# Block 2: the norms, the output ahead of each and the first two panels behind it in two halves of the tokens

## The chip, the cores and the metric

The kernel runs on one core of a Trainium2 chip. Its engines are PE (matrix engine; its weight loads are shown apart as PEld), DVE (vector), ACT (scalar), POOL and SP, which here only issues transfers; the trace calls the queue of an engine DVEq, SPq and so on. The metric is the device time of one execution in microseconds (us), as the median of several.

## The reference

Two stacks of two transformer layers each, on 512 tokens of width 1024. The first (with 256 context tokens, three attentions and a gate) ends with a norm. The second is what the change touches. Each of its layers:

```python
h = rmsnorm_2(x, norm_mix_g[l]) * (1.0 + sc1) + sh1
u = h @ w_in[l]
# four mixers: attention with decay, pooling, retention, convolution
mix = jnp.concatenate([y_fox, y_pool, y_ret, y_conv], axis=-1)
x = x + g1 * (mix @ w_out[l])

h = rmsnorm_2(x, norm_ffn_g[l]) * (1.0 + sc2) + sh2
f = (jax.nn.silu(h @ ffn_w1[l]) * (h @ ffn_w3[l])) @ ffn_w2[l]
x = x + g2 * f
```

and behind both layers `rmsnorm_2(x, final_g)`. The norm divides each token by the root of the mean of its squares over all 1024 features.

## The kernel before

Activations lie feature by feature: `xl` is 128 partitions (features) by `KC` = 8 chunks by 512 tokens. All weights come as panels of 128 output features (512 KB) through SP. Each is rounded by ACT (`round_panel`, L1176, which waits until a slot of `split` is given back; there are 3), and its rest is made by DVE (`rest`, L1715) or, for the input panels of the second stack, by POOL (`rest2`, L1031). A product is three matmuls for each chunk (high by high, high by low, low by high; `product`, L2216), so a panel of 8 chunks is 24 matmuls of 512 columns. In the first stack an output's weights are two panels of 6 chunks in two slots (L2180 to L2204), in the feed-forward's second product (`w2`) two panels of 6 and 5 chunks in three slots (`W2_CUT`, L2469 to L2483).

The order of the work is written out by hand for each engine; engines meet only through semaphores, and each takes its instructions strictly in its order.

There are five places where a norm stands between an output and what follows: place 0 between the stacks (with two norms at once, the first stack's last and the second's first), place 1 from the mixers' output to the feed-forward in layer 0, place 2 from layer 0 to layer 1, place 3 as place 1 in layer 1, place 4 the last norm. At each of them:

- DVE adds every output to `xl` (`update`, L1937; L1710 in the first stack); ACT squares it (`square`, L1330; `square1`, L1148), POOL adds up the squares of chunks 0 to 6 (`add_square`, L1017).
- PE sums over the features with one-column matmuls (`sum_squares`, L2006; at place 0 `sum_both_squares`, L2017, with 48 passes), first what POOL added up, then the square of the last chunk.
- ACT takes the root, DVE the reciprocal (`over_roots`, L1516), PE spreads it over all partitions (`spread_roots`, L2042).
- `norm_split` (DVE, L1722) multiplies each chunk into `hm2`, a ring of four; `shifted` (ACT, L1337) adds the shift and rounds it into `hs`; the rest of the even chunks is made by DVE (L1736), of the odd ones by POOL (`split_odd`, L1075).
- `first_products` (PE, L2228) multiplies two panels at once with each chunk as it comes. All further panels run alone.
- `norm` (DVE, L1521) is the last norm; SP sends the result in one transfer (L1005).

At places 0 and 2 the first panel gives the forget gate: ACT takes it (L1367), forms its logarithm (L1468 to L1473), DVE a running sum (L1849 to L1853), and then DVE starts 62 steps of the convolution (L1762). Ahead of ACT's take stand, at place 0, POOL's rest of the third panel and four memsets (`pads_done`, L1087 to L1090), and DVE's final norm of the first stack (L1750).

## Time and profile before

| what | us |
|---|---|
| median of three runs | 2600.06 (2599.46 to 2600.43) |
| the profiled execution, whole | 2602.91 |
| its span, first to last instruction | 2601.1 |
| PE busy | 2467.2 (95%) |
| PE weight loads busy | 1989.6 (76%) |
| DVE, ACT, POOL busy | 1328.9 (51%), 938.6 (36%), 538.6 (21%) |

The span is shorter than the execution by 1.8 us. The trace gives for each instruction its start in the span and its length; matmuls are pipelined, so their lengths overlap and only their distances add up. In the groups of rows below, "x8" is the count of instructions in a row, and the bracket says how long the engine stood idle before and who released it. The granted clock is the share of full speed (2.4 GHz) that PE was given; 0.5 is 1.2 GHz.

### The profile page before, as it was taken

The page shows a single profiled execution, that of the slowest core. Times are in us where ns is not written, and L with a number is a line of the kernel's source. Part 1 is how long each engine was busy: PE and PEld are TensorE (multiplying, and loading weights), DVE is VectorE, ACT ScalarE, POOL GpSimd, SP SyncE. Part 2 cuts the span into 40 slices and gives each one's busy share as a digit, 9 for nine tenths or more (in the row PEclk, how much of TensorE's full clock was granted, in tenths as well). Part 3 has the DMA queues.
Part 4 walks back from the last instruction along what each step waited for, and adds up shares of the span by engine and source line. Part 5 has one row for each costly group of instructions (what it writes and reads, how often), then busy time and mean ns, then how long its engine had stood idle before and what let it go on. Part 6 is the DMA issues. An engine that isn't in the chain of part 4 may idle for free.

```text
span 2601.1 us, 37185 instructions
## 1 busy us (share of the span) xinstructions
PE 2467.2 (95%) x14408; PEld 1989.6 (76%) x14408; DVE 1328.9 (51%) x2663; ACT 938.6 (36%) x1686; POOL 538.6 (21%) x512
## 2 busy tenths in 40 slices
PE   6999999999998999999999999999999999999997
PEld 4777877878886678778777657888887667788886
DVE  4567757665306663666717644333334854433333
ACT  4354254452323542545334333222224333322221
POOL 2211222212343122222364231000003232000001
PEclk9899999999998999999999999999999999999999
DMA  6301422125124034132433112323323212223322
GB/s 265 133 1 52 178 76 88 64 86 189 55 94 161 2 122 154 38 130 110 176 103 122 49 54 68 98 79 116 95 80 101 67 49 73 82 82 106 104 77 70
DMA packets 64383, 250.31 MB, mean 96 GB/s; under 512 B 7888, under 2 KB 9424, under 8 KB 54736
## 3 DMA queue, kind: packets, MB, share of 16 engines
q1 hardware_dynamic: 59920, 234.26, 26.9%
q0 software_dynamic: 3776, 13.63, 1.6%
q8 instruction: 115, 1.88, 0.3%
q14 instruction: 60, 0.49, 0.1%
q10 hardware_dynamic: 512, 0.03, 0.0%
HBM read 243.67 MB, written 4.19 MB: 95 GB/s over the span
## 4 chain that ended last, share of the span: by engine, by line
PE 85%; DVE 7%; ACT 4%; issue 2%; DVEq 1%; DMA 0%; POOL 0%; ACTq 0%; SPq 0%
PE ps L2221 37%; PE ps L2078 20%; PE ps L2200 6%; PE ps L560 5%; PE ps L588 5%; PE ps L628 4%; DVE ps L1762 2%; ACT probs L777 2%; PE ps L2059 1%; PE ps L2166 1%; PE ps L2047 0%; PE ps L566 0%; DVE ps L694 0%; PE ps L602 0%; PE ps L638 0%
## 5 line engine op out<-in xcount | busy, mean ns | idle before, releaser
L2221 PE MATMUL ps<-h_split,split_panels 128*128 128x512 f32 x3120 | 742.3, 397 | 10.5 <-DVE h_split L1736 10.0
L2221 PEld LDWEIGHTS ps<-h_split,split_panels 128*128 128x128 f32 x3120 | 590.9, 191 | 146.9 <-issue 25.1
L2078 PE MATMUL ps<-h_split_first,split_panels_first 128*128 128x512 f32 (+1 forms) x2880 | 576.1, 358 | 16.8 <-DVE h_split_first L1649 8.8
L2078 PEld LDWEIGHTS ps<-h_split_first,split_panels_first 128*128 128x128 f32 x2880 | 470.7, 193 | 96.5 <-issue 10.9
L1014 POOL TENSOR_TENSOR split_panels_first<-panels_first,split_panels_first 128x1024 fp32r<-128x1024 f32 (+1 forms) x104 | 232.9, 2240 | 579.4 <-ACT split_panels_first L1174 579.4
L1720 DVE TENSOR_TENSOR split_panels<-panels,split_panels 128x1024 fp32r<-128x1024 f32 (+2 forms) x171 | 191.0, 1117 | 311.6 <-ACT split_panels L1182 309.7
L1182 ACT ACTIVATE split_panels<-panels 128x1024 fp32r<-128x1024 f32 (+2 forms) x210 | 204.2, 974 | 351.3 <-PE ps L2221 350.4
L1601 DVE SCALAR_TENSOR_TENSOR ps<-modulation_panels,silu_c,ps 128x256 f32<-128x256 f32 x480 | 225.2, 487 | 29.7 <-issue 1.3
L2221 PE MATMUL ps<-ffn_hidden_split,split_panels 128*128 128x512 f32 x1056 | 240.0, 389 | 0.0
L2221 PEld LDWEIGHTS ps<-ffn_hidden_split,split_panels 128*128 128x128 f32 x1056 | 198.2, 188 | 41.2
L1022 POOL TENSOR_TENSOR probs<-probs 128x512 f32<-128x512 f32 (+1 forms) x36 | 52.8, 1467 | 781.5 <-ACT probs L1335 781.5
L588 PE MATMUL ps<-matrices,probs 128*128 128x128 f32 x1104 | 154.2, 284 | 23.5 <-ACT probs L777 23.1
L588 PEld LDWEIGHTS ps<-matrices,probs 128*128 128x128 f32 x1104 | 121.6, 143 | 67.3 <-ACT probs L777 44.0
L560 PE MATMUL ps<-qkv 64*128 64x256 f32 (+2 forms) x1168 | 161.4, 388 | 8.3 <-DVE probs_turned L706 2.2
L1174 ACT ACTIVATE split_panels_first<-panels_first 128x1024 fp32r<-128x1024 f32 (+1 forms) x104 | 104.6, 1007 | 119.5 <-PE ps L2200 97.5
L2200 PE MATMUL ps<-gated_rounded,split_panels_first 128*128 128x512 f32 x576 | 144.2, 359 | 3.1 <-ACT gated_rounded L1255 2.4
L560 PEld LDWEIGHTS ps<-qkv 64*128 64x128 f32 x1168 | 103.5, 191 | 48.7 <-issue 23.9
L1034 POOL TENSOR_TENSOR split_panels<-panels,split_panels 128x1024 fp32r<-128x1024 f32 x39 | 95.6, 2453 | 197.0 <-ACT split_panels L1182 197.0
L777 ACT ACTIVATE probs<-ps,row_min 128x512 f32<-128x512 f32 (+6 forms) x192 | 122.6, 649 | 31.3 <-DVE row_min L694 19.7
L805 POOL TENSOR_TENSOR wide_weights<-matrices,row_weight 128x64 f32<-128x64 f32 x240 | 65.3, 294 | 317.0 <-DVE row_weight L712 292.9
L1234 ACT ACTIVATE qkv<-ps 128x512 f32<-128x512 f32 x38 | 36.6, 963 | 247.1 <-PE ps L2078 247.1
L683 DVE TENSOR_REDUCE row_min<-ps 128x1 f32<-128x768 f32 (+5 forms) x144 | 94.1, 671 | 52.2 <-PE ps L560 50.2
(254 smaller groups left out, 2692.7 us busy)
## 6 DMA issues: line engine op xcount, KB each, us to landing
modulation_panels<-in_ada SPq DMA_DIRECT2D x64, 1024.0 KB, 5.0
panels<-in_w SPq DMA_DIRECT2D x88, 512.0 KB, 3.5
panels_first<-in_in SPq DMA_DIRECT2D x72, 512.0 KB, 5.8
panels<-in_in SPq DMA_DIRECT2D x42, 512.0 KB, 3.5
panels_first<-in_out SPq DMA_DIRECT2D x32, 384.0 KB, 3.0
panels<-in_w SPq DMA_DIRECT2D x32, 384.0 KB, 3.0
panels<-in_w SPq DMA_DIRECT2D x32, 320.0 KB, 2.9
panels<-in_out SPq DMA_DIRECT2D x16, 512.0 KB, 3.6
```

The costliest lines, as they stand in the source:

```text
L560: last[e] = nc.tensor.matmul(scores_at(u, e, u["w"][e])[:, col:col + z - a], u["q"][e], u["k"][e][:, a:z], start=True, stop=True, skip_gro ...
L588: ins = nc.tensor.transpose(bank(ev["bank"], at0, at0 + P), probs[:, u["probs_at"], e, col:col + P], ident)
L628: ins = nc.tensor.matmul(bank(b, 0, P)[rows_of(e)], v, turned_slot(ev, 512)[:, at0:at0 + P], start=ev["first"] and j < 2, stop=ev["last"] ...
L777: nc.scalar.activation(probs[:, u["probs_at"], e, 0:w], scores_at(u, e, w), ACT.Exp, bias=row_min[:, s:s + 1], scale=scale, accum_out=row_ ...
L1014: nc.gpsimd.tensor_tensor(flat1(n, 1), raw1[:, n % RAW1, 0:main_size(n)], flat1(n, 0).bitcast(F32), ALU.subtract).then_inc(rest1_done, 1)
L1174: A_(flat1(n, 0), raw1[:, n % RAW1, 0:main_size(n)], ACT.Copy).then_inc(rounded1, 1)
L1182: A_(flat(n, 0), raw[:, n % RAW, 0:panel_size(n)], ACT.Copy).then_inc(rounded, 1)
L1601: ins = V.scalar_tensor_tensor(out=adding if c < KC - 1 else products(k)[:, i, :], in0=w[:, c, :], scalar=v, in1=adding, op0=ALU.mult, op1 ...
L1720: V.tensor_tensor(flat(n, 1), raw[:, n % RAW, 0:panel_size(n)], flat(n, 0).bitcast(F32), ALU.subtract).then_inc(rest_done, 1)
L2078: ins = mm(at0, split1[:, s, w, c, :], hs1[:, h, c, lo:e], start=c == 0 and i == 0, stop=c == KC - 1 and i == 2)
L2200: ins = mm(bank(OUT_BANKS[j][o % 2], 0, e), split1[:, n % SPLIT1, w, c, :], u[:, uc, lo:lo + e], start=uc == 0 and i == 0, stop=uc == MIXC ...
L2221: ins = mm(out, split[:, n % SPLIT, a, c - base, :], moving(b, c), start=first and i == 0 and j == 0, stop=last and i == len(chunks) - 1 a ...
```

## The change

At all five places the 512 tokens are taken as two halves of 256, `h` = 0 and 1:

- The last output (`last_output`) runs all its matmuls on half 0 (256 columns), then on half 1, into two banks. Between the halves come the sums of chunks 0 to 6; at 3/8 of half 1 the sum of the last chunk's squares of half 0, at 3/4 of it the spread of half 0. It needs both panels of the output from its start.
- The last chunk's update, square, root and reciprocal are done per half (`update_half`, `square_half`, `root_half`, `over_half_roots`); those of half 1 lie between the chunks of the norm's half 0.
- `norm_split`, `shifted`, `split_odd` and `first_products` go through all eight chunks of half 0 and then of half 1. The third panel's rounding is put behind chunk 5 of half 0, its rest behind the whole norm (at places 1 and 3 both were ahead of it). At place 2 the second panel is rounded behind the root of half 0, and its rest stands on DVE between the reciprocal and the first chunk. The table of Silu is loaded behind `shifted`.
- At place 0 the sum for the second norm is formed from squares weighted with root(w^2 + eps), made once at the start, so one sum is enough ahead of the norm; the plain sum for the first stack's own norm (16 passes) goes between the halves of the first products, its spread behind them. POOL's `rest2(0, 0)` is moved one step back.
- The last norm goes by halves too, and the result leaves in six transfers: 4 and 4 chunks of half 0, then 2, 2, 2 and 2 of half 1.

```diff
-            sp.wait_ge(result_ready, KC)
-            sp.dma_start(out, xl[:, :, :]).then_inc(result_out, 16)
-            sp.wait_ge(result_out, 16)
+            pieces = [(0, 0, 4), (0, 4, 8), (1, 0, 2), (1, 2, 4), (1, 4, 6), (1, 6, 8)]
+            for h, a, e in pieces:
+                sp.wait_ge(result_ready, KC * h + e)
+                sp.dma_start(out[:, a:e, half_cols(h)], xl[:, a:e, half_cols(h)]).then_inc(result_out, 16)
+            sp.wait_ge(result_out, 16 * len(pieces))
...
+            def square_half(r, h, q, x_count, scale=1.0):
+                if h == 0:
+                    act.wait_ge(sq_added, 6 * q + KC - 3)
+                    act.wait_ge(xh_ready, r + 1)
+                else:
+                    act.wait_ge(x_ready, x_count)
+                A_(squares2[:, (KC - 1) % 2, half_cols(h)], xl[:, KC - 1, half_cols(h)], ACT.Square, scale=scale).then_inc(
+                    sq_ready if h else sq_half, 1)
+            def root_half(r, h):
+                act.wait_ge(sums_half, 2 * r + h + 1)
+                A_(roots[:, 2 * h:2 * h + 2], bank(T_BANK, 2 * h, 2 * h + 2), ACT.Sqrt, bias=EPS if r else tiny[:, 0:1],
+                   scale=1.0 / DM).then_inc(std_half, 1)
...
+            def shifted(r, shift, panel, q, x_count, scale=1.0):
+                for h in range(2):
+                    s = half_cols(h)
+                    for c in range(KC):
+                        act.wait_ge(hm_ready, hm_count(r, h, c))
+                        if c % 2:
+                            A_(hm2[:, c % 4, s], hm2[:, c % 4, s], ACT.Identity, bias=shift(c))
+                            act.drain()
+                            A_(hs[:, 0, c, s], hm2[:, c % 4, s], ACT.Copy).then_inc(hh_ready, 1)
+                        else:
+                            A_(hs[:, 0, c, s], hm2[:, c % 4, s], ACT.Identity, bias=shift(c)).then_inc(hh_ready, 1)
+                        if (h, c) == (0, 1):
+                            square_half(r, 1, q, x_count, scale)
+                        if (h, c) == (0, 3):
+                            root_half(r, 1)
+                            if r == 0:
+                                act.wait_ge(plain_added, KC - 3)
+                                plain_square(KC - 1)
+                        if (h, c) == (0, 5):
+                            round_panel(*panel)
+                        if r == 0 and (h, c) == (1, 1):
+                            act.wait_ge(plain_summed, 1)
+                            A_(roots[:, 4:8], bank(S_BANK, 0, 4), ACT.Sqrt, bias=EPS, scale=1.0 / DM).then_inc(plain_std, 1)
...
+                r = norm_no(l, True)
+                for c in range(KC - 1):
+                    square(DEPTH + r, c, NX1 + l * OUTS2)
                     round_panel(N_IN2 + c + SPLIT, l)
-                root(4 + l * 2, SEQ // P)
+                square_half(r, 0, DEPTH + r, None)
+                root_half(r, 0)
+                shifted(r, lambda c: mod2[:, l, 24 + c:25 + c], (FFN_AT + SPLIT - 1, l), DEPTH + r, NX1 + l * OUTS2 + KC)
                 load_table(ACT.Silu)
-                shifted(4 + l * 2, lambda c: mod2[:, l, 24 + c:25 + c])
...
+            def update_half(r, h, at0, gate, ready, count):
+                s, c = half_cols(h), KC - 1
+                dve.wait_ge(ready, count)
+                old = xl[:, c, s] if r else x1[:, c, s]
+                V.scalar_tensor_tensor(out=xl[:, c, s], in0=bank(at0)[:, s], scalar=gate, in1=old,
+                                       op0=ALU.mult, op1=ALU.add).then_inc(x_ready if h else xh_ready, 1)
...
+            def norm_split(r, gain, shift, at0, gate, count, panels):
+                over_half_roots(r, 0)
+                for p in panels[:-1]:
                     rest(*p)
+                for h in range(2):
+                    s = half_cols(h)
+                    dve.wait_ge(rstd_half, 2 * r + h + 1)
+                    for c in range(KC + 1):
+                        if c < KC:
+                            if c >= 5 and c % 2:
+                                dve.wait_ge(*h_done2(r, h, c - 4))
+                            V.scalar_tensor_tensor(out=hm2[:, c % 4, s], in0=xl[:, c, s], scalar=gain(c), in1=rstd_half_in(h),
+                                                   op0=ALU.mult, op1=ALU.mult).then_inc(hm_ready, 1)
+                        if c % 2:
+                            dve.wait_ge(hh_ready, hm_count(r, h, c - 1))
+                            V.scalar_tensor_tensor(out=hs[:, 1, c - 1, s], in0=hm2[:, (c - 1) % 4, s], scalar=shift(c - 1),
+                                                   in1=hs[:, 0, c - 1, s].bitcast(F32), op0=ALU.add, op1=ALU.subtract).then_inc(h_even, 1)
+                        if (h, c) == (0, 1):
+                            update_half(r, 1, at0, gate, out_ready, count)
+                        if (h, c) == (0, 4):
+                            over_half_roots(r, 1)
+                        if r == 0 and (h, c) == (1, 4):
+                            dve.wait_ge(plain_std, 1)
+                            V.reciprocal(roots[:, 4:8], roots[:, 4:8]).then_inc(plain_over, 1)
+                dve.wait_ge(*h_done2(r, 1, KC - 1))
+                rest(*panels[-1])
...
-            dve.drain()
-            norm(3 + 2 * DEPTH, xl, lambda c: vec("final_g", c), xl, result_ready)
+            over_half_roots(r, 0)
+            for h in range(2):
+                s = half_cols(h)
+                dve.wait_ge(rstd_half, 2 * r + h + 1)
+                for c in range(KC):
+                    V.scalar_tensor_tensor(out=xl[:, c, s], in0=xl[:, c, s], scalar=vec("final_g", c), in1=rstd_half_in(h),
+                                           op0=ALU.mult, op1=ALU.mult).then_inc(result_ready, 1)
+                    if (h, c) == (0, 1):
+                        update_half(r, 1, 4, mod2[:, DEPTH - 1, 40 + KC - 1:40 + KC], out_ready, out1_done + DEPTH * OUTS2)
+                    if (h, c) == (0, 5):
+                        over_half_roots(r, 1)
...
+            def sum_most(q):
+                pe.wait_ge(sq_added, 6 * q + KC - 2)
+                    mm(bank(T_BANK, t, t + 1), square_sum2[:, P * t:P * t + P], ones[:, 0:1], start=t == 0, stop=False, skip_group_check=True)
+            def sum_last(r, h):
+                if h:
+                    pe.wait_ge(sq_ready, KC * (DEPTH + r) + KC)
+                else:
+                    pe.wait_ge(sq_half, r + 1)
+                for t in (2 * h, 2 * h + 1):
+                    ins = mm(bank(T_BANK, t, t + 1), squares2[:, (KC - 1) % 2, P * t:P * t + P], ones[:, 0:1], start=False, stop=True,
+                             skip_group_check=True)
+                ins.then_inc(sums_half, 1)
+            def spread_half(r, h):
+                pe.wait_ge(over_half, 2 * r + h + 1)
+                for i in range(2):
+                    ins = mm(rstd_half_in(h)[:, P * i:P * i + P], roots[:, 2 * h + i:2 * h + i + 1].to_broadcast([P, P]), ident,
+                             start=True, stop=True)
+                ins.then_inc(rstd_half, 1)
+            def last_output(r, q, at, factors, first_panel=0, first_used=None):
+                for h in range(2):
+                    for i, (w, moving) in enumerate(factors):
+                        ins = mm(bank(at[h])[:, half_cols(h)], w, moving[:, half_cols(h)], start=i == 0, stop=i == len(factors) - 1)
+                        if h and i + 1 == first_panel:
+                            ins.then_inc(first_used, 1)
+                        if h and i == len(factors) * 3 // 8:
+                            sum_last(r, 0)
+                        if h and i == len(factors) * 3 // 4:
+                            spread_half(r, 0)
+                    if h:
+                        ins.then_inc(out_ready, 1)
+                    else:
+                        ins.then_inc(out_half2, 1)
+                        sum_most(q)
...
+            pe.wait_ge(rest1_done, N_MAIN)
+            pe.wait_ge(x_ready, KC * DEPTH - 2)
+            last_output(0, DEPTH, (4, 3), [(split1[:, part, w, c, :], u[:, MIXC // 2 * part + c, :]) for part in range(2)
+                                           for c in range(MIXC // 2) for w, u in ((0, u_hi), (1, u_hi), (0, u_lo))],
+                        3 * MIXC // 2, out_half)
...
+            def first_products(banks, panels, r, signals, l):
+                for h in range(2):
+                    s = half_cols(h)
+                    for c in range(KC):
+                        pe.wait_ge(*h_done2(r, h, c))
+                        for at0, n, signal in zip(banks, panels, signals):
+                            if (h, c) == (0, 0):
+                                split_wait(n, l)
+                            for j, (a, b) in enumerate(((0, 0), (0, 1), (1, 0))):
+                                ins = mm(bank(at0)[:, s], split[:, n % SPLIT, a, c, :], hs[:, b, c, s], start=c == 0 and j == 0,
+                                         stop=c == KC - 1 and j == 2)
+                            if (h, c) == (1, KC - 1):
+                                ins.then_inc(signal, 1)
+                        if (h, c) == (0, 1):
+                            sum_last(r, 1)
+                        if (h, c) == (0, 4):
+                            spread_half(r, 1)
+                        if r == 0 and (h, c) == (0, KC - 1):
+                            sum_plain()
...
+                        if (f, c) == (1, KC - 1):
+                            r, i = norm_no(l + 1, False), PER2 - len(W2_CUT)
+                            split_wait(i, l)
+                            split_wait(i + 1, l)
+                            last_output(r, DEPTH + r, (3, 4), [(split[:, (i + j) % SPLIT, w, k - a, :], act_part(b, k))
+                                                               for j, (a, e) in enumerate(W2_CUT) for k in range(a, e)
+                                                               for w, b in ((0, 0), (0, 1), (1, 0))],
+                                        3 * W2_CUT[0][1], w2_used)
+                            break

```

## Rows read from the trace of the kernel before

**Rows 1.** The page: the chain that ended last, shares of the span by engine

```profile
PE 85%; DVE 7%; ACT 4%; issue 2%; DVEq 1%; DMA 0%; POOL 0%; ACTq 0%; SPq 0%
```

**Rows 2.** Timeline of place 2: start us, us, engine, line, operation, [idle before <- releaser]

```profile
1976.90 0.95 PE L2010 MATMUL ps<-matrices,probs 128*128 128x1 f32 x8
1977.10 0.75 DVE L1940 SCALAR_TENSOR_TENSOR x_latent<-ps,mod_second,x_latent 128x512 f32<-128x512 f32 x1 [1.03 <-PE ps L2221]
1978.56 0.97 PEld L2013 LDWEIGHTS ps<-matrices,probs 128*128 128x128 f32 x8 [0.80 <-ACT probs L1335]
1981.29 1.41 DVE L1732 SCALAR_TENSOR_TENSOR probs<-x_latent,gain_second,ps 128x512 f32<-128x512 f32 x2 [1.25 <-PE ps L2047]
1983.72 13.54 PE L2221 MATMUL ps<-h_split,split_panels 128*128 128x512 f32 x48 [2.48 <-DVE h_split L1736]
1996.62 0.68 ACT L1367 ACTIVATE values_forgetting<-ps,layer_vectors 4x512 f32<-4x512 f32 x1 [5.15 <-PE ps L2221]
```

**Rows 3.** A stretch behind place 2, PE alone: stretch, us, busy (count), granted clock

```profile
1983.70:1989.00 5.30, 5.28 (x13) 0.52 0.00 0
```

**Rows 4.** Groups by shape: line, engine, operation, count | busy us, mean ns

```profile
L1643 DVE SCALAR_TENSOR_TENSOR probs<-qkv,gain_first,ps 128x256 f32<-128x256 f32 x16 | 7.6, 473 | 0.0
...
L1298 ACT ACTIVATE h_split_first<-probs,mod_first 128x256 fp32r<-128x256 f32 x8 | 3.9, 493 | 0.0
...
L1079 POOL TENSOR_TENSOR h_split<-probs,h_split 128x512 fp32r<-128x512 f32 x16 | 20.6, 1289 | 57.1 <-ACT h_split L1346 57.1
L1045 POOL TENSOR_TENSOR h_split_first<-probs,h_split_first 128x768 fp32r<-128x768 f32 x8 | 14.6, 1830 | 35.6 <-ACT h_split_first L1295 35.6
```

**Rows 5.** Timeline of place 1

```profile
1608.00 0.95 PE L2010 MATMUL ps<-matrices,probs 128*128 128x1 f32 x8
...
1610.60 1.23 DVE L1720 TENSOR_TENSOR split_panels<-panels,split_panels 128x1024 fp32r<-128x1024 f32 x1 [1.64 <-ACT split_panels L1182]
1616.89 1.04 DVE L1736 SCALAR_TENSOR_TENSOR h_split<-probs,mod_second,h_split 128x512 fp32r<-128x512 f32 x1
...
1628.25 0.60 ACT L1494 ACTIVATE probs<-ps 128x512 f32<-128x512 f32 x1 [5.34 <-PE ps L2221]
```

**Rows 6.** Two streams on the chain (start us, us), and a group of the page

```profile
583.99 8.44 PE ps L2078 x48
952.10 5.71 PE ps L2078 x24
...
L2221 PEld LDWEIGHTS ps<-h_split,split_panels 128*128 128x128 f32 x3120 | 590.9, 191 | 146.9 <-issue 25.1
```

**Rows 7.** Place 0: one line of the chain in order of time, then the timeline

```profile
1351.82 8.39 PE ps L2200 x36
...
1352.93 1.85 POOL L1014 TENSOR_TENSOR split_panels_first<-panels_first,split_panels_first 128x768 fp32r<-128x768 f32 x1
...
1382.60 2.39 POOL L1034 TENSOR_TENSOR split_panels<-panels,split_panels 128x1024 fp32r<-128x1024 f32 x1
1386.10 0.68 ACT L1367 ACTIVATE values_forgetting<-ps,layer_vectors 4x512 f32<-4x512 f32 x1 [4.83 <-POOL decay_of_keys L1090]
1391.77 0.63 ACT L1473 ACTIVATE values_forgetting<-values_forgetting 4x512 f32<-4x512 f32 x1
1392.89 0.67 DVE L1849 SCALAR_TENSOR_TENSOR values_forgetting<-values_forgetting 4x512 f32<-4x512 f32 x1
```

**Rows 8.** Timeline of place 4; SPq is the queue of SyncE

```profile
2584.69 0.95 PE L2010 MATMUL ps<-matrices,probs 128*128 128x1 f32 x8
...
2594.47 0.35 SPq L1005 DMA_DIRECT2D out_features<-x_latent  x1
```

**Rows 9.** The page: DMA issues, KB each, median us to landing

```profile
panels<-in_in SPq DMA_DIRECT2D x42, 512.0 KB, 3.5
...
panels<-in_w SPq DMA_DIRECT2D x32, 320.0 KB, 2.9
...
out_features<-x_latent SPq DMA_DIRECT2D x1, 2048.0 KB, 6.2
```

250 lines of the change are left out of this document (123 added, 127 removed).

## The prediction

> **What bounds the kernel now.** I read the shares of the chain that ended last first: 85% of it is the matrix engine (PE) [rows 1], so time is gained only where PE waits, or at the two ends. The change touches five places: place 0, between the blocks; places 1 and 3, mixing to feed-forward; place 2, layer 0 to layer 1; place 4, the end. The timeline of place 2 shows the pattern [rows 2]. The last output is done at 1976.90, where the sums of squares begin on PE. Update (DVE), square (ACT), sum (PE, 1978.56), root (ACT), reciprocal (DVE) and spread (PE) follow strictly after one another; the norm starts on DVE at 1981.29 and the first product at 1983.72: 6.8 us, of which PE is at sums and spreads for about half. Then PE pays again: the granted clock is 0.52 over the first 5.3 us of the products, nearly all of it at 1.2 GHz [rows 3]. In that time some 12 matmuls are done where 23 would be at full speed, a loss of 2.5 us. Place 1 is alike: the sums start at 1608.00, and the first two panels are through at about 1628.75 (ACT takes the first of them at 1628.25, and three matmuls are still to come behind it) [rows 5]. Place 4 is a chain without cover: 2584.69 to the end of the span at 2601.1 [rows 8]. Place 0 starts at 1351.82 + 8.39 = 1360.2 [rows 7]. J below is the instant at which the last output is done, and J' the same after the change.
>
> **Halved matmuls.** No stream of 256-column matmuls with a load each is in the trace. A stream of pairs (512 and 256 columns, a load each) takes 8.44 us for 48, 0.352 a pair; 24 of 512 columns take 5.71, or 0.238 each [rows 6]. So a half costs 0.114, half of a whole, as long as its own weight load fits under it. The nearest row for the load alone is eight loads with one-column matmuls behind them: 0.97 us, the last one's own 0.19 included, so (0.97 - 0.19) / 7 = 0.111 apart [rows 2]. That just fits. Bounds: 0.111, the load alone, up to 0.19, the length of one load record [rows 6], if none were hidden. I take 0.115, since the pairs are the nearer row, and nothing for the halving.
>
> The Trainium skill speaks against this ("TensorE: Matmul & The Clock Gate", "Back-to-back issue gap"): sustained spacing 131 ns at 512 columns and 81 ns at 128, so two halves would cost clearly more than one whole. By interpolation that is about 98 ns a half, an estimate from that page, and 65 ns more for each split matmul, 22 us for the 342 of them. The row of 0.238 for 512 columns disagrees with its first figure already.
>
> **The last output in halves (places 1 to 4).** PE's own work is the same, but its 24 one-column and spread passes now lie elsewhere: eight passes between the halves (0.95), four behind 3/8 of the second half (0.45), four spreads behind 3/4 of it (0.5). So the output ends 1.9 us later, at J' = J + 1.9. The prices are of one-column passes and spreads 0.111 each [rows 2]. Covered: from the end of the first half, update and square take 1.0 (two ops of 256 columns, 0.473 and 0.493 [rows 4]), and the sum is asked for 0.95 + 1.2 us in: no wait. From the end of the sums (1978.56 + 0.97) to the norm on DVE (1981.29) it was 1.8, the eight spreads (1.0 at least) among it: 0.8 for root and reciprocal, and nine half matmuls (1.0) cover them. Small waits are left: at places 1 and 3 DVE has the rest of a panel (1.23 [rows 5]) ahead of the first half's update and may still be at it, so the update starts up to 1.2 late and PE waits some 0.3. J' = J + 2.2 there, and with hand-overs J + 2.0 at places 2 and 4.
>
> **The norm in halves.** DVE can start 0.55 us before J'. Prices at 256 columns: DVE 0.473, ACT 0.493, and POOL's rest 0.75, extrapolated from 1.289 at 512 and 1.830 at 768 [rows 4]. The loop of two chunks: DVE norms one chunk (0.51 with the hand-over), ACT shifts it (0.53), DVE makes its rest (0.41 to 0.56: at full width such an op took 1.04 with POOL at work [rows 5], where the update took 0.75 [rows 2]), then the next two. That is 1.45 to 1.6 us for two chunks, where at full width it was up to 1.41 + 1.04 = 2.45 [rows 2, 5]; I take 1.6, since POOL is at work in every such loop. PE needs 12 x 0.115 = 1.4 for the same two chunks, so **the producers now set the pace, not PE**. First half: 4 x 1.6, and 1.7 for the panel's rounding (1.0), the second half's square, root and update: 8.1. Second half: 4 x 1.6 and 1.2 for the last odd chunk's way over ACT's copy (no longer than its shift, 0.49) and POOL (0.75): 7.6. So POOL is done at J' - 0.55 + 15.7 = J' + 15.1, PE's last chunk at J' + 15.9. The clock matters little now: PE has slack of 0.2 a pair and some at each hand-over. Only if it fell for 4 to 5 us would PE lag by about 2, and it would catch up more than half of it.
>
> **Places 1 and 3.** The rest of the third panel was made before the norm (1610.60, 1.23) [rows 5]; now it stands behind it on DVE: J' + 15.1 + 1.3 = J' + 16.4, 0.5 later than PE's last chunk. The third panel starts at J + 2.2 + 16.4 = J + 18.6; before, 1628.75 - 1608.00 = 20.75. Gain 2.1 each. The table load for Silu is also put behind the norm, 1.5 us on ACT, which ends as the first product arrives: nothing. What SP loads behind that panel is asked for some 15 us later, but is used five panels (28 us) on.
>
> **Place 2.** Two rests stand in the way: that of panel 1 (1.23) is on DVE between the reciprocal and the first chunk, and can only be rounded once the first w2 panel is given back (2.2 before J'). DVE starts at J' + 0.35, 0.9 later than elsewhere. ACT takes the first product at J' + 16.6 = J + 18.6; before 1996.62 - 1976.90 = 19.7 [rows 2]. Gain 1.1. Everything to the attention follows from that instant (logarithm, then the convolution on DVE), so it arrives whole.
>
> **Place 0.** Here the change adds a wait. The last output now needs both of its panels before it starts. The second panel's slot is given back by the output before (PE starts the last output at 1351.82), then ACT rounds and POOL makes the rest (1352.93, 1.85), ready at 1354.8 [rows 7]. Before, it was wanted 4.2 us into the output. Now PE stands for 3.1 us. Everything on PE is behind it. J' = J + 1.9 + 3.1 = J + 5.0. The plain sum (16 passes, 1.8) goes between the halves and ACT waits for it after two chunks: 2 us more, POOL's end at J' + 17.1. Then as before rest (2.39), memsets (1386.07 less 1384.99, 1.1), ACT's take: J' + 20.7, and the logarithm 6.3 later (1386.10 to 1392.40) [rows 7]: J + 32.0. Before, DVE went on at 1392.89, J + 32.7. Gain 0.7. What went: 48 passes, most of them at the slow clock; what came in: the stall and the slower producers. The loads behind x_ready start 5 us later; a panel of 512 KB lands in 3.5 us at the median, the 2048 KB of the result in 6.2 [rows 9], and this one is due 4 us after its issue: bounds 0 to 2 us, and I take 0 by the row of its own size. DVE's final norm (5.36) starts at J' + 19.3 and is done before the logarithm.
>
> **Place 4.** J' = J + 2.0 = 2586.7. DVE starts 0.75 before it, does two chunks (0.43 each, 0.473 less the overlap that 1.41 for two whole ones shows), update to J' + 0.7, four chunks, reciprocal, two chunks to J' + 3.5, second half 8 x 0.43 to J' + 7.0. The last of six transfers is 256 KB. Before, one of 2048 KB ran from its issue at 2594.47 to the end of the span, 6.6 us, 6.2 of them to landing [rows 8, 9]. The nearest in size, 320 KB, lands in 2.9 [rows 9]: J' + 7.0 + 2.9 + 0.4 = 2597.0. Gain 4.1. Pieces cut to runs of 256 tokens, and six in one queue, are not in the trace. All six together move what the one moved in at most 6.2 us, the first of them from J' + 1.7 on, so even at that rate they are through at J' + 8 or 9. Bounds: 3 (the queue backs up by 1 us) to 4.7 (a smaller piece lands sooner).
>
> **Sum.** 0.7 + 2.1 + 1.1 + 2.1 + 4.1 = 10.1 us. Profiled execution 2602.91 (span 2601.1 and 1.8 around it) to 2592.8; the median of the runs, 2600.06, is 2.85 below the profiled one, so 2589.95, say 2589.9. At 1.45 a pair each of places 0 to 3 gains 1.2 more: 2585. At 1.75, 1.2 less: 2594.6.
>
> **The rivals.** Weight loads that do not hide (slower): some 300 half matmuls of the last outputs and 384 of the first products. On the last outputs each nanosecond counts; on the first products only what is above the producers' 0.133. At 0.19 that is 300 x 0.075 + 384 x 0.057 = 44 us, time 2634. It decides from about 0.14 on, where 300 x 0.025 + 384 x 0.007 = 10.2 eat the gain. Against it stand the 0.352 a pair and 0.111 a load. The page named above would come out on this side: chance 0.06. Producers slower than I have it (hand-overs, POOL and DVE in each other's way, the loads at place 0): 1.8 to 1.9 a pair, 1.6 to 2.4 less at four places, 2597: 0.19. Faster producers, 1.45 a pair and the full 4.7 at the end: 2584: 0.13. That it does not do what it says, the clock still dropping, at place 0 because PE now stands for 3.1 us just ahead of dense work: 2 us there, 0.7 at the others, 2594: 0.07. My forecast: 0.55.
>
> **How the numbers follow.** Likeliest time 2589.9. The range of 2583 to 2598 takes in faster and slower producers and leaves out the weight loads and the tails. Within 0.2% (5.2 us, about what a measurement of this kernel tells from no change) begins at 2594.9: faster takes my forecast, the faster producers, the clock case and a quarter of the slower producers, 0.80; same most of the rest of those, 0.14; slower 0.06.
>
> **What would show it.** Right: granted clock 1.0 through places 1 to 3; the norm's first chunk on DVE before PE's last half matmul; chunks 1.6 us a pair; PE waiting for POOL and DVE within the first products; 3.1 us of waiting for the last panel's rest at place 0; last transfer issued 10 us behind J. Wrong: half matmuls over 0.13 apart, a PE wait inside the last output's second half, a transfer at the end landing 4 us after its issue.

## The result, and the profile after

The changed kernel takes 2582.29 us (median of five runs, 2578.97 to 2586.53), the kernel before 2599.66 us beside it (2599.46 to 2600.43): a ratio of 0.9935, with a 95% interval of 0.9921 to 0.995. It is faster by 17.4 us where 10.1 were forecast, and lies 0.7 us below the range. The profiled execution takes 2582.29 us, with a span of 2580.4.

The page of the changed kernel: the slices of the granted clock, and the chain that ended last. Above it stands the slice row of the kernel before.

```profile
PEclk9899999999998999999999999999999999999999
```

```profile
PEclk9999999999998999999999999999999999999999
...
PE 82%; DVE 7%; ACT 5%; issue 3%; POOL 2%; DVEq 1%; DMA 1%; ACTq 1%; SPq 0%; POOLq 0%
```

POOL is new on the chain with 2% [rows 1 has 0%], 47 us. Only 6.7 of them are rests of the halved norms (L1103), for which PE now waits. The larger part are rests of the first stack's panels (L1035, 20.1) and squares (L1046 and L1053, 15.2), most of them under the last outputs ahead of place 0, where the chain runs over POOL instead of PE and an output takes 8.40 us as before. The timeline of place 1 answers [rows 5]:

```profile
1599.32 0.88 DVE L1810 SCALAR_TENSOR_TENSOR probs<-x_latent,gain_second,ps 128x256 f32<-128x256 f32 x2 [1.25 <-PE ps L2142]
1600.92 0.98 PE L2382 MATMUL ps<-h_split,split_panels 128*128 128x256 f32 x6 [1.04 <-DVE h_split L1814]
...
1608.48 0.86 DVE L1810 SCALAR_TENSOR_TENSOR probs<-x_latent,gain_second,ps 128x256 f32<-128x256 f32 x2
1608.98 0.51 ACT L1395 ACTIVATE h_split<-probs,mod_second 128x256 fp32r<-128x256 f32 x1
1609.53 0.49 DVE L1814 SCALAR_TENSOR_TENSOR h_split<-probs,mod_second,h_split 128x256 fp32r<-128x256 f32 x1 [0.18 <-ACT h_split L1395]
1609.94 0.86 DVE L1810 SCALAR_TENSOR_TENSOR probs<-x_latent,gain_second,ps 128x256 f32<-128x256 f32 x2
...
1613.39 0.74 POOL L1103 TENSOR_TENSOR h_split<-probs,h_split 128x256 fp32r<-128x256 f32 x1 [0.72 <-ACT h_split L1393]
1614.16 1.23 DVE L1795 TENSOR_TENSOR split_panels<-panels,split_panels 128x1024 fp32r<-128x1024 f32 x1 [1.22 <-POOL h_split L1103]
```

```profile
1615.44 0.73 PE L2365 MATMUL ps<-h_split,split_panels 128*128 128x512 f32 x2 [0.27 <-DVE split_panels L1795]
```

The last output is done at 1599.87, so the norm starts 0.55 ahead of its end, two chunks follow two chunks by 1.46 (1608.48, 1609.94), and the third panel starts at 1615.44. At place 2, ACT's take is at 1981.67, 25.2 us behind DVE's update with the seventh output (1956.46); before it was 27.0 ([rows 2] has the take at 1996.62, the update was at 1969.61):

```profile
1966.16 0.87 DVE L1810 SCALAR_TENSOR_TENSOR probs<-x_latent,gain_second,ps 128x256 f32<-128x256 f32 x2
...
1981.67 0.68 ACT L1425 ACTIVATE values_forgetting<-ps,layer_vectors 4x512 f32<-4x512 f32 x1 [1.53 <-PE ps L2382]
```

Place 0: POOL's rest of the second panel, PE's wait for it, and the granted clock behind the wait (columns as in [rows 3], with all engines):

```profile
1346.06 1.81 POOL L1035 TENSOR_TENSOR split_panels_first<-panels_first,split_panels_first 128x768 fp32r<-128x768 f32 x1
...
1347.92 0.79 PE L2152 MATMUL ps<-gated_rounded,split_panels_first 128*128 128x256 f32 x2 [2.97 <-POOL split_panels_first L1035]
```

```profile
1600.90:1606.20 5.30, 5.08 (x39) 4.71 (x39) 3.74 (x10) 4.52 (x11) 2.21 (x3) 1.00 0.00 0
1347.90:1353.70 5.80, 5.78 (x27) 5.78 (x28) 0.00 (x0) 2.01 (x2) 4.77 (x3) 0.50 0.00 0
```

The upper row is place 1, at full clock. The lower is place 0: 27 half matmuls in 5.8 us, at 1.2 GHz from the first.

**Where the time went.** I cut both traces at instants that exist in both: DVE's update with the seventh of eight outputs ahead of each place, DVE's first operation of the convolution, and the end of the span. Place 1 and 3 are taken together with the feed-forward part behind them. The two profiled executions stand first; the other rows are experiments, told below, and a_same is the changed kernel once more.

| us | to place 0 | place 0 | mixing, layer 0 | place 1 + FFN | place 2 | mixing, layer 1 | place 3 + FFN | place 4 |
|---|---|---|---|---|---|---|---|---|
| before | 1351.86 | 46.16 | 204.67 | 366.93 | 38.47 | 201.69 | 367.63 | 23.70 |
| after | 1344.99 | 47.30 | 199.83 | 364.34 | 36.68 | 203.38 | 364.59 | 19.31 |
| a_same | 1353.48 | 46.22 | 199.62 | 364.35 | 36.68 | 201.64 | 364.59 | 19.32 |
| b_setup | 1346.94 | 46.17 | 201.80 | 366.76 | 38.23 | 201.97 | 366.90 | 23.74 |
| b_shift | 1343.05 | 46.19 | 200.61 | 367.64 | 38.35 | 201.67 | 367.60 | 23.70 |
| b_fill | 1350.43 | 46.18 | 200.74 | 365.31 | 36.70 | 200.13 | 365.29 | 24.99 |
| b_mix_fill | 1346.63 | 46.20 | 197.55 | 367.56 | 38.34 | 198.78 | 366.86 | 23.69 |
| a_by_panels | 1344.16 | 42.38 | 199.51 | 364.34 | 36.65 | 201.61 | 364.63 | 19.31 |
| a_one_transfer | 1346.93 | 47.31 | 199.92 | 364.36 | 36.67 | 203.32 | 364.62 | 22.80 |
| a_rest_at_once | 1349.09 | 47.36 | 199.76 | 364.35 | 37.26 | 200.17 | 364.35 | 19.29 |
| a_no_copy | 1350.92 | 43.24 | 200.02 | 362.87 | 35.24 | 200.25 | 362.86 | 19.30 |
| a_early | 1347.68 | 42.35 | 200.68 | 364.94 | 37.66 | 201.33 | 365.21 | 18.90 |
| a_mix_fill | 1349.92 | 42.39 | 198.29 | 364.33 | 36.67 | 197.07 | 364.64 | 19.30 |

From the first two rows: the five places gain -1.14 + 2.59 + 1.79 + 3.04 + 4.39 = **10.7 us**. The other 10.0 us lie in three stretches in which the change does nothing: 6.9 ahead of place 0, 4.8 in the mixing of layer 0, and -1.7 in that of layer 1. So the question for the chip was what these 10 us are.

### The profile page after: what moved, and what is told of

It is laid out like the page before. It is cut to its first block, busy times and chain, and to the rows that moved or that the text cites. A ratio compares the mean times of both kernels' runs of the same rounds, so it can differ in the third digit from the quotient of the medians.

```text
span 2580.4 us, 37996 instructions
## 1 busy us (share of the span) xinstructions
PE 2453.9 (95%) x14734; PEld 1992.7 (77%) x14734; DVE 1338.6 (52%) x2730; ACT 950.7 (37%) x1745; POOL 542.1 (21%) x527
## 4 chain that ended last, share of the span: by engine, by line
PE 82%; DVE 7%; ACT 5%; issue 3%; POOL 2%; DVEq 1%; DMA 1%; ACTq 1%; SPq 0%; POOLq 0%
PE ps L2365 34%; PE ps L2219 21%; PE ps L567 5%; PE ps L595 5%; PE ps L635 4%; PE ps L2341 4%; DVE ps L1850 2%; ACT probs L784 2%; PE ps L2152 1%; PE ps L2200 1%; POOL split_panels_first L1035 1%; PE ps L2307 1%; PE ps L573 0%; DVE ps L701 0%; PE ps L2382 0%
## 5 line engine op out<-in xcount | busy, mean ns | idle before, releaser
L2365 PE MATMUL ps<-h_split,split_panels 128*128 128x512 f32 x2928 | 691.2, 395 | 4.1 <-ACT values_forgetting L1425 2.8
L2365 PEld LDWEIGHTS ps<-h_split,split_panels 128*128 128x128 f32 x2928 | 549.8, 189 | 130.7 <-issue 16.5
L1035 POOL TENSOR_TENSOR split_panels_first<-panels_first,split_panels_first 128x1024 fp32r<-128x1024 f32 (+1 forms) x104 | 233.3, 2243 | 574.6 <-ACT split_panels_first L1220 574.6
L2365 PE MATMUL ps<-ffn_hidden_split,split_panels 128*128 128x512 f32 x990 | 225.1, 389 | 0.0
L2365 PEld LDWEIGHTS ps<-ffn_hidden_split,split_panels 128*128 128x128 f32 x990 | 185.8, 188 | 38.6
L1046 POOL TENSOR_TENSOR probs_turned<-probs_turned,probs 128x512 f32<-128x512 f32 x30 | 41.8, 1394 | 771.2 <-ACT probs L1382 771.2
L2341 PE MATMUL ps<-gated_rounded,split_panels_first 128*128 128x512 f32 (+1 forms) x552 | 136.4, 357 | 3.1 <-ACT gated_rounded L1301 2.4
```

Of the source, the lines that this page charges most:

```text
L1035: nc.gpsimd.tensor_tensor(flat1(n, 1), raw1[:, n % RAW1, 0:main_size(n)], flat1(n, 0).bitcast(F32), ALU.subtract).then_inc(rest1_done, 1)
L2341: ins = mm(bank(OUT_BANKS[j][o % 2], 0, e), split1[:, n % SPLIT1, w, c, :], u[:, uc, lo:lo + e], start=uc == 0 and i == 0, stop=uc == MIXC ...
L2365: ins = mm(out, split[:, n % SPLIT, a, c - base, :], moving(b, c), start=first and i == 0 and j == 0, stop=last and i == len(chunks) - 1 a ...
```

## The experiments

Two theories on the 10 us. **A**: where PE waits or has little to do, the granted clock may or may not fall to 1.2 GHz behind it; which of these falls happen is dealt anew in each execution. **B**: the change removes something fixed there.

### a_same: the changed kernel once more

> The changed kernel as it is, once more, on this chip. Against the kernel before it gained 17.4 us where 10.1 were forecast, and its runs lie 7.6 us apart (2578.97 to 2586.53) where those of the kernel before lie 1.0 apart. Theory A (the clock is dealt anew): the surplus comes from stretches outside the five places in which the granted clock is 1.2 GHz in one kernel's execution and 2.4 in the other's. Then the intervals inside the places (from the end of the last output to the third panel, about 17.5 us at place 1) repeat to 0.3 us here, the total lies somewhere in 2577 to 2588, a longer run has a lower mean clock, and the stretches at 1.2 GHz outside the places are not all the same as in the first profile (those at about 130, 670, 780, 1030, 1245, 1430, 2030 and 2130 us). Theory B (the surplus is fixed work saved): the same stretches and the same total to 0.5 us.

2582.71 us (2580.04 to 2587.76, four runs); before 2596.75 beside it, now from 2591.74 to 2603.05 in 25 runs, ratio 0.9945 (0.9924 to 0.9967). The table: places 1 to 4 repeat to 0.01 us (with their FFN), but the stretch ahead of place 0 takes 1353.48 instead of 1344.99, with the same code. Theory A holds, and B falls. Another chip is no rival: a_by_panels to a_no_copy below ran on one chip with the same code up to place 0, and took 1344.16 to 1350.92 us to it. The kernel before scatters too, by 11 us, and a slower run has a lower mean clock: over its 41 later runs on three chips the two have a correlation of -0.8, from 2588.78 us at 0.979 to 2601.0 and more at 0.972. Its five runs beside the first comparison lie within 1 us; why they lie so close is not shown. Their mean of 2599.9 is 2.4 above that of the 25 (2597.4).

Place 0 is dealt anew as well. The same wait of 2.97 stands there, but in the 5.8 us behind it 36 half matmuls run instead of 27:

```profile
1356.40:1362.20 5.80, 5.79 (x36) 5.80 (x37) 0.00 (x0) 1.99 (x2) 4.77 (x3) 0.71 0.00 0
```

### b_setup: the kernel before with the change's set-up operations

```diff
+ act.wait_ge(tiny_set, 1)
+ A_(weights_of_squares[:, :], weights_of_squares[:, :], ACT.Sqrt, bias=EPS)
...
+ V.tensor_tensor(weights_of_squares[:, :], vec("final_w", 0, KC), vec("final_w", 0, KC), ALU.mult)
```

> The kernel before with nothing but the small set-up operations of the change (a product of 8 columns on DVE, its root on ACT, a tile of 8 columns; nothing reads them). In the trace of the changed kernel 7.1 us of the gain are there by 1230 us, before any of its five places; this asks whether the set-up code carries them. Theory A (the clock is dealt anew by any small displacement): the total moves by some us in either direction, 2593 to 2606, and the difference is seen in stretches at 1.2 GHz, not in work. Theory B (the set-up itself saves them, for instance by another alignment): 2593 and the same stretches gone as in the changed kernel (about 85, 230 and 345 us). Theory C (nothing of either): 2600 and the same stretches as before.

2595.51 us (2591.49 to 2600.63), ratio 0.9996 (0.9985 to 1.0007). The set-up does not carry the gain: theory B's saving of 7 us is excluded by the interval, which leaves 3.9 us at most. Theory A expected the single executions to move, which they do (1346.94 ahead of place 0), but of its "in either direction" the median shows nothing either: over ten runs the deals even out.

### b_shift: the kernel before, started later

```diff
+ for i in range(5):
+     pool.memset(silu_rows, 0.0)
+     pool.drain()
  pool.memset(silu_rows, 0.0).then_inc(silu_zeros, 1)
+ pool.wait_ge(silu_zeros, 1)
+ pool.sem_inc(late_start, 1)
...
+ sp.wait_ge(late_start, 1)
```

> The kernel before with five more memsets of 0.3 us ahead of the first transfer, so that all starts about 1.6 us later and nothing else is changed. Theory A (the clock is dealt anew by any small displacement): the total is not 1.6 us above the kernel before; it lies anywhere from 2593 to 2607, with a mean clock other than 0.971. Theories B and C (the losses belong to fixed places of the program): 2601.7, mean clock 0.971, the same stretches at 1.2 GHz 1.6 us later.

2595.35 us (2590.85 to 2599.24), ratio 0.9995 (0.9982 to 1.0007). The profiled execution is 12.3 us shorter in its span than that of the kernel before (2588.8 against 2601.1), although it starts 2.5 us later (its first transfer at 3.26 instead of 0.75). Here is one stretch of the same work, first in the kernel before, then 6 us earlier in b_shift, then in the changed kernel (there the 10 us start about 2 us earlier in the work):

```profile
225.00:235.00 10.00, 7.70 (x56) 5.42 (x53) 5.21 (x19) 3.73 (x11) 1.63 (x6) 0.83 0.01 2
```

```profile
219.00:229.00 10.00, 7.71 (x65) 5.59 (x64) 5.75 (x22) 3.96 (x11) 1.63 (x6) 1.00 0.01 2
```

```profile
219.00:229.00 10.00, 7.30 (x67) 4.77 (x66) 5.31 (x23) 5.49 (x16) 2.18 (x8) 1.00 0.01 2
```

With the code before, the clock falls in this stretch in one execution and not in the other. So the 6.9 us are not the change's: over five traces with the code before, the way to place 0 takes 1347.8 us in the mean, over eight with the changed code 1348.4. PE's first matmul starts at 16.13 to 18.77 in them, so of the 10.4 us between the shortest and the longest way at most 2.6 are the start.

### b_fill: idle matmuls in the waits of places 1 to 3

```diff
+ def fill(n, q):
+     for i in range(n):
+         still = act_part(0, 0) if q == 4 else mix_part(0, 0)
+         mm(bank(5), still[:, 0:P], still, start=True, stop=True)
...
+ if q in (3, 4, 5):
+     fill(4, q)
  pe.wait_ge(sq_ready, KC * q + KC)
...
  sum_squares(3 + l * 2, SEQ // P)
+ fill(3, 3)
  spread_roots(4 + l * 2, SEQ // P)
+ fill(9, 3)
...
```

Place 2 gets `fill(3, 4)` and `fill(9, 4)` in the same way: 16 idle matmuls at each of the three places.

> The kernel before, with 16 idle matmuls of 512 columns (0.238 us each, 3.8 us in all) put where PE only waits at places 1, 2 and 3: 4 ahead of the last square's sums, 3 ahead of the spreads, 9 behind them; they write a bank that nobody reads. It keeps PE at work through the gap and changes nothing else. The prediction had 2.5 us of each of these places as the price of products at 1.2 GHz behind a gap. If so: granted clock 1.0 in the first products, the first product is taken by ACT 17.2 us after the last output's end at place 2 instead of 19.7, and the kernel takes 2592.5 (3 x 2.5 less), up to 1 us more where a filler is still in the way. Rival: the pace of the producers bounds these products anyhow, so that the clock costs under 1 us a place: 2598 or more.

2593.5 us (2584.82 to 2596.47, ten runs), ratio 0.9979 (0.9967 to 0.9991), which is 5.5 us less where 7.5 were expected (the two medians lie 3.3 apart, the means 4.5, and the interval of 2.3 to 8.6 us holds all of these; the places below decide). Place 2, the stretch that [rows 3] shows at 0.52 (here from the first long stream on), and ACT's take:

```profile
1976.80:1982.10 5.30, 4.99 (x21) 3.85 (x22) 4.61 (x7) 5.05 (x8) 2.61 (x2) 1.00 0.00 0
```

```profile
1974.16 2.32 PE L2010 MATMUL ps<-ffn_hidden_split 128*128 128x512 f32 x9
...
1976.88 1.63 PE L2229 MATMUL ps<-h_split,split_panels 128*128 128x512 f32 x6 [0.40 <-DVE h_split L1736]
...
1987.90 0.68 ACT L1367 ACTIVATE values_forgetting<-ps,layer_vectors 4x512 f32<-4x512 f32 x1 [3.26 <-PE ps L2229]
```

ACT's take comes 17.95 us behind the last output's end (1969.95), where 17.2 were expected and 19.7 stood before. The fall is gone at all three places. Against the other traces of the code before, place 1 with its FFN is 1.9 us shorter (365.31, where the other four have 367.2 in the mean), place 2 1.6 (36.70 and 38.35), place 3 2.0 (365.29 and 367.2), 5.5 in all: the clock's price was **1.6 to 2.0 us a place**, not 2.5. At full clock PE waits for the producers within these products (0.23 for POOL at 1978.74), which it did not at 1.2 GHz. Place 4, which has no filler, took 1.3 us longer in this trace: a fall of the clock met its sums and spreads, and eight spreads take 2.07 instead of 1.16. And at place 2 the filled kernel is as fast as the halved one, 36.70 and 36.68. There the halves bring nothing that a running PE does not; at places 1 and 3 they bring 0.7 to 1.0 more. A reason would be that the rest of the third panel stands behind the norm there and no longer ahead of it; that wasn't tried by itself.

### a_by_panels: place 0 without the wait

Shortened; the new order stands in a function of its own. In it the sum for the first half stands behind 5/9 of the second panel's second half, and the spread behind its last matmul.

```diff
- pe.wait_ge(rest1_done, N_MAIN)
+ pe.wait_ge(rest1_done, N_MAIN - 1)
...
- for h in range(2):
-     for i, (w, moving) in enumerate(factors):
+ for a, e in ((0, first_panel), (first_panel, n)):
+     if a:
+         pe.wait_ge(rest1_done, N_MAIN)
+     for h in range(2):
+         for i, (w, moving) in enumerate(factors[a:e], a):
```

> The changed kernel, with place 0's last output made panel by panel: first panel for both halves of the tokens, then second panel for the first half, then for the second half (72 half matmuls as before; only their order). The second panel is then not wanted until 4.2 us into the output. The prediction put 3.1 us of waiting here; the trace of the changed kernel shows 2.97, and behind it 5.8 us (in the second execution 3.3) in which a half matmul takes 0.213 instead of 0.118. If the wait is the cause of both: no wait ahead of the output, granted clock 1.0 from its start, norm on DVE 10.4 us behind the start of the wait (72 x 0.117 + 1.9 for the passes) instead of 14.1 to 15.2, place 0 shorter by 3.7 to 4.8, kernel 2578 to 2579 against 2582.5. Rival: what follows (the rest of the second panel on POOL, the tables and loads asked for behind x_ready) sets the end of place 0 anyhow, and it gets under 1 us shorter.

2579.69 us (2574.45 to 2582.64), ratio 0.9936 (0.9917 to 0.9954). Place 0 takes 42.38, 4.9 less than in the first trace of the changed kernel and 3.8 less than in the second, where 3.7 to 4.8 were expected. The output runs at full clock, and the norm starts 10.4 us behind its first matmul (1343.96):

```profile
1344.20:1350.00 5.80, 5.80 (x52) 5.80 (x51) 0.71 (x1) 3.99 (x5) 5.80 (x5) 1.00 0.00 0
```

```profile
1354.37 0.87 DVE L1810 SCALAR_TENSOR_TENSOR probs<-x_latent,gain_second,ps 128x256 f32<-128x256 f32 x2 [0.92 <-PE ps L2142]
```

### a_one_transfer: the result in one piece

```diff
- for h, a, e in pieces:
-     sp.wait_ge(result_ready, KC * h + e)
-     sp.dma_start(out[:, a:e, half_cols(h)], xl[:, a:e, half_cols(h)]).then_inc(result_out, 16)
+ sp.wait_ge(result_ready, 2 * KC)
+ sp.dma_start(out, xl[:, :, :]).then_inc(result_out, 16)
```

> The changed kernel, with the result leaving in one transfer of 2048 KB behind the last chunk instead of six. The prediction had the last of six landing 2.9 us behind its issue, the one 6.2. If so, place 4 gets 3.3 us longer. Rival: six transfers of 256-token runs in one queue are no faster in all than the one, and the end is set by the queue: under 1 us.

2587.0 us (2582.43 to 2590.87), place 4 22.80 against 19.31: 3.5 us, as expected. Its one transfer is issued at 2578.94 and the span ends at 2585.9. The DMA issues of the changed kernel over its last 11 us show that six in a queue don't hold each other up:

```profile
out_features<-x_latent SPq DMA_DIRECT2D x2, 512.0 KB, 3.0
out_features<-x_latent SPq DMA_DIRECT2D x4, 256.0 KB, 2.8
```

Of the 4.4 us of place 4, 3.5 are thus the transfers and 0.9 the halves.

### a_rest_at_once: the third panel's rest without its wait

```diff
- dve.wait_ge(*h_done2(r, 1, KC - 1))
  rest(*panels[-1])
```

> The changed kernel, without DVE's wait for POOL's last chunk ahead of the rest of the third panel. In the trace PE waits 0.27 us for that rest at place 1 (and 0.68 at place 2, where ACT's take of the first product is the event that counts). If the wait is what puts it so late: rest on DVE about 1.2 us earlier, third panel on PE 0.3 earlier at places 1 and 3, nothing at place 2. Rival: the rest beside POOL's last chunk slows POOL or itself (1.23 to more than 2), and PE's last chunk comes later.

One run, 2583.58 us. Place 1 with its FFN stays at 364.35, place 3 is 0.2 us shorter, place 2 0.6 us longer: the rival. DVE's rest and POOL's last chunk now run side by side, and POOL's takes 1.29 instead of 0.74:

```profile
1983.83 1.21 DVE L1795 TENSOR_TENSOR split_panels<-panels,split_panels 128x1024 fp32r<-128x1024 f32 x1
...
1984.34 1.29 POOL L1103 TENSOR_TENSOR h_split<-probs,h_split 128x256 fp32r<-128x256 f32 x1 [0.72 <-ACT h_split L1393]
```

### a_no_copy: one ACT operation less for each odd chunk

```diff
- if c % 2:
-     A_(hm2[:, c % 4, s], hm2[:, c % 4, s], ACT.Identity, bias=shift(c))
-     act.drain()
-     A_(hs[:, 0, c, s], hm2[:, c % 4, s], ACT.Copy).then_inc(hh_ready, 1)
- else:
-     A_(hs[:, 0, c, s], hm2[:, c % 4, s], ACT.Identity, bias=shift(c)).then_inc(hh_ready, 1)
+ A_(hs[:, 0, c, s], hm2[:, c % 4, s], ACT.Identity, bias=shift(c)).then_inc(hh_ready, 1)
```

> The changed kernel, with the shift of the odd chunks left out of their rests: ACT rounds them in one operation like the even ones, instead of shift, drain and copy, so the rests of the odd chunks are wrong. It asks which engine sets the pace of 1.46 us for two chunks, where the prediction had 1.6 and DVE. In a pair ACT is busy 0.51 + 0.49 + 0.42 = 1.42, DVE 0.86 + 0.49 = 1.35, PE 12 x 0.117 = 1.40. If ACT sets it: 1.40 or DVE's 1.38 a pair, and places 1 to 3 each 0.4 shorter. If DVE or the hand-overs between DVE and ACT set it: 1.46 stays to 0.02.

One run, 2576.57 us. The kernel leaves out the shift in the rests of the odd chunks. Neither expectation is met whole. The pace stays at 1.46 (1608.12, 1609.58, 1611.03), as in the last line of the expectation, with ACT now idle 0.55 in each pair:

```profile
1608.12 0.86 DVE L1805 SCALAR_TENSOR_TENSOR probs<-x_latent,gain_second,ps 128x256 f32<-128x256 f32 x2
...
1608.63 0.91 ACT L1390 ACTIVATE h_split<-probs,mod_second 128x256 fp32r<-128x256 f32 x2 [0.55 <-DVE probs L1805]
1609.17 0.49 DVE L1809 SCALAR_TENSOR_TENSOR h_split<-probs,mod_second,h_split 128x256 fp32r<-128x256 f32 x1 [0.19 <-ACT h_split L1390]
1609.58 0.87 DVE L1805 SCALAR_TENSOR_TENSOR probs<-x_latent,gain_second,ps 128x256 f32<-128x256 f32 x2
```

So in the even run of the loop the ring DVE, ACT, DVE sets the pace: 0.86 for two chunks, 0.19 of waiting for ACT, 0.41 until the next. Yet places 1 to 3 are 1.4 to 1.7 us shorter. At place 1 the first half takes 6.75 us instead of 7.69 (1601.37 to 1608.12), the second 6.61 instead of 7.12. In the first half ACT also has the square, the root and the panel's rounding (1.04), and DVE's wait behind that rounding falls from 1.23 to 0.71: there ACT is in part the bound. In the second half, at an unchanged pace, the 0.5 is what the last odd chunk's way over ACT is shorter. I had put the whole difference down to one engine; it changes between the halves.

Place 0 takes 43.24 here, 3 to 4 us less than in the other traces with the wait. The wait is there (2.96), but the clock does not fall behind it, and 49 half matmuls run in the 5.8 us:

```profile
1353.80:1359.60 5.80, 5.75 (x49) 5.76 (x50) 0.48 (x1) 2.52 (x3) 4.84 (x3) 1.00 0.00 0
```

Of the 3 to 4 us, the missing copies may be 1.4 to 1.7, as at the other places; that is an estimate.

### a_early: spreads at 5/8, update behind four chunks

```diff
- if h and i == len(factors) * 3 // 4:
+ if h and i == len(factors) * 5 // 8:
      spread_half(r, 0)
...
- if (h, c) == (0, 1):
+ if (h, c) == (0, 3 if r else 1):
      update_half(r, 1, at0, gate, out_ready, count)
...
- if (h, c) == (0, 4):
+ if (h, c) == (0, 6 if r else 4):
      spread_half(r, 1)
```

> The kernel of a_by_panels with, at places 1 to 4, the spreads of the first half behind 5/8 of the second half instead of 3/4, and the second half's update on DVE behind four chunks of the norm instead of two (square, sum, root and spreads move with it). In the trace of the changed kernel the reciprocal is done at 2568.2 and the spreads are asked for at 2569.16 only. If the start of the norm sets the end of these places: it starts 0.9 us earlier (8 x 0.117), each of places 1 to 4 gets 0.8 to 1.0 shorter, kernel 3.5 below a_by_panels' 2579.7. Rival: the update, two chunks later against the last output's end, holds up the second half (square, sum, root, reciprocal and spreads stand behind it), and ACT's rounding of the panel now meets them: no gain, or up to 0.5 us longer a place.

2581.72 us (2580.54 to 2584.9), ratio 0.994 (0.9916 to 0.9964), no better than a_by_panels. Places 1 and 3 are 0.6 us longer, place 2 1.0, place 4 0.4 shorter: the rival, and a little more than its 0.5. At place 2 the norm does not even start earlier: 9.7 us behind the seventh output's update (1955.66 to 1965.37), as in the changed kernel (1956.46 to 1966.16), since DVE still has the rest of a panel ahead of it. And the second half's spreads come late on PE, behind seven chunks of products, so that DVE waits 1.51 for them:

```profile
1965.37 0.87 DVE L1810 SCALAR_TENSOR_TENSOR probs<-x_latent,gain_second,ps 128x256 f32<-128x256 f32 x2
...
1973.39 0.60 PE L2142 MATMUL ps<-matrices,norm_roots 128*128 128x128 f32 x4
...
1974.03 0.87 DVE L1810 SCALAR_TENSOR_TENSOR probs<-x_latent,gain_second,ps 128x256 f32<-128x256 f32 x2 [1.51 <-PE ps L2142]
```

### a_mix_fill and b_mix_fill: idle matmuls in the mixing

```diff
  part(m, 0, 4)
+ fill(12, 2)
  scores_pe(pe, U[1], o)
```

> The kernel of a_by_panels with 12 idle matmuls of 512 columns (2.9 us) in each layer's mixing, where PE stands for 3.2 us ahead of the second unit's scores (at 1424.8 us in the changed kernel); they write a bank that nobody reads. In every trace so far, of either kernel, the granted clock falls to 1.2 GHz behind this wait, for 6.8 to 10.2 us in each layer. If idling is what brings the clock down there and PE is what bounds the stretch: clock 1.0 through it, mixing 3 to 4.5 us shorter in each layer, kernel 2571 to 2574. Rival: this stretch is bound by ACT's and DVE's work on the scores, so that the clock costs nothing there: under 1 us a layer.

> The kernel before, with the same 12 idle matmuls in each layer's mixing. The same as for a_mix_fill, 3 to 4.5 us a layer or under 1. Besides, it is one more trace of the code before: the stretch of layer 0's mixing from 130 us behind its start has so far fallen to 1.2 GHz in all four kernels with the code before and in two of six with the changed code. If these falls come by chance (theory A), it may or may not show; if the code before brings them, it shows.

a_mix_fill takes 2573.81 us (2570.23 to 2574.49), ratio 0.9903 (0.9875 to 0.9931): it beats both kernels. b_mix_fill takes 2587.42 in its one run. PE's wait and the stretch behind it in layer 0, first in a_by_panels, then in a_mix_fill (whose 12 us start with the fillers; the same work comes 5.7 us later there). Each fence has PE's first matmuls behind the wait, then 12 us with all engines:

```profile
1422.28 1.23 PE L567 MATMUL ps<-projected 64*128 64x256 f32 x4 [3.17 <-ACT probs L784]
1424.00:1436.00 12.00, 12.00 (x62) 7.64 (x59) 8.26 (x20) 4.75 (x12) 2.39 (x1) 0.82 0.07 11
```

```profile
1428.01 0.70 PE L567 MATMUL ps<-projected 64*128 64x256 f32 x4 [0.52 <-ACT probs L784]
1424.00:1436.00 12.00, 11.48 (x61) 7.48 (x60) 10.82 (x26) 4.16 (x12) 1.70 (x2) 1.00 0.11 44
```

The fall behind the wait is gone in both layers of both kernels. Layer 0's mixing is 1.6 us shorter with the changed code (another fall, at 1550 us, came in its place) and 4.4 with the code before; layer 1's 4.6 and 2.6, each against the mean of the traces without the filler (199.9 and 202.0; 201.7 and 201.4). The mean is 3.3, between the bounds of 3 to 4.5 that I had expected; the single ones lie from 1.6 to 4.6, by the other falls that each trace got.

And b_mix_fill does not show the fall from 130 us into layer 0's mixing that the other four traces of the code before had: it is no property of that code.

## Why the prediction was wrong in its number, and why its sum came out near

**The step that failed** is the last step of the sum, from the profiled execution to the time: "the median of the runs, 2600.06, is 2.85 below the profiled one, so 2589.95". It takes the rest of the program as a constant that both kernels share. It isn't: the way to place 0, the same work in all, took 1343.05 to 1353.48 us in 13 traces, mostly by the falls of the clock that each execution got. The median before came from runs 2.4 us above this kernel's mean on the next chip, and the changed kernel's nine runs average 2583.1, 14.3 below that mean of 2597.4. Of the 7.3 us over the forecast 10.1, 2.3 are thus the base; whether that was chance or the chip is not shown. The nine runs' mean is just inside the range, and the five runs' median 0.7 outside it. The range had no term for it, and the scatter of the changed kernel alone (7.6 us) would have asked for one; it could not be seen in three runs within 1 us.

**What remains.** The places give 10.7 and the medians differ by 14 to 17. Layer 0's mixing is 2.1 us shorter in the mean of seven traces with the changed code than in four with the code before (199.9 and 202.0, both without fillers in the mixing), layer 1's 0.3 longer. The time that each trace spent at 1.2 GHz in these stretches accounts for most of it. In layer 1 both kernels take the same at the same time there: with about 7 us at 1.2 GHz 200.13 before and 200.17 and 200.25 after, with 10 us 201.67 to 201.97 and 201.33 to 201.64, with 14 us 203.32 and 203.38. In layer 0 the seven traces of the changed code all have about 7 us, and so has b_fill with the code before, 200.74 against 199.9; the other three have 10 to 17. So at most some 0.8 us of layer 0's mixing may be the change's, and where the other 3 us between 10.7 and 14.3 come from stays open.

**Place by place.** Means over the traces in which the place is unaltered:

| us gained | forecast | the two profiled | means |
|---|---|---|---|
| place 0 | 0.7 | -1.1 | -0.9 |
| place 1 | 2.1 | 2.6 | 2.9 |
| place 2 | 1.1 | 1.8 | 1.7 |
| place 3 | 2.1 | 3.0 | 2.6 |
| place 4 | 4.1 | 4.4 | 4.4 |
| sum | 10.1 | 10.7 | 10.7 |

That the sum came out within 0.6 is luck in part: place 0 was forecast 1.6 too high, and places 1 to 3 together 1.9 too low.

**Halved matmuls: right.** 0.117 each on the last outputs (three in 0.352) where 0.115 was taken. The rival of weight loads that don't hide is out: a half costs half of the whole, 0.238. The estimate of 98 ns for a half, worked out from the Trainium skill ("TensorE: Matmul & The Clock Gate", "Back-to-back issue gap"), does not hold here, neither in its size nor as a price above half of a whole.

**The last output and the norm's start: right.** At place 1, J = 1591.92 + 24 x 0.238 = 1597.6; the output ends at 1599.87 (J + 2.2 forecast, 2.2 read), the norm starts 0.55 ahead of that.

**The pace: mis-sized.** 1.6 us a pair was taken and 1.46 measured, the lower bound. The term was the rest on DVE: its 0.56 came from a full-width row that was slow beside POOL (1.04 against 0.75 [rows 5, 2]); at half width it takes its 0.49 (0.41 to the next) with POOL at work or not. The norm's two halves took 7.7 and 7.1 where 8.1 and 7.6 were forecast, so the third panel starts at J' + 15.6 instead of 16.4. That is the 0.5 to 0.8 us too little at places 1 to 3. The case of faster producers, with 2584, had the pace right.

**The clock at places 1 to 3: right that it stays at 1.0**, though its price was 1.6 to 2.0 us and not 2.5.

**Place 0: the wait was right, what follows it wrong.** 2.97 us of waiting were forecast as 3.1. But the sum had the clock at 1.0 behind it, and the half clock there, which stood among the rivals at 2 us, came in both traces of the changed kernel and in four of the five traces that have the wait (not in a_no_copy): 27 half matmuls at 0.213 instead of 0.117 are 2.6 us in the one, 0.29 x 5.8 / 0.5 = 3.4 us at half clock, or 1.7, in the other. Without that place 0 would have gained 1.5 to 1.7. A fall behind a wait just ahead of dense work should have been in the sum and not in a case of 0.07. The prediction also has most of the 48 passes before "at the slow clock"; the trace has 30 of them at full clock, and the fall at 1364.2.

**Place 4: right**, 4.4 at the upper part of 3 to 4.7, the pieces landing in 2.8 to 3.0. The last output ended 0.3 later than forecast, and DVE was through 6.2 us behind it instead of 7.0; the last piece was issued 8.5 us behind J, not the 10 that the signs named.
